# The order of 512-column and 256-column products in the feed-forward projections of a three-layer transformer kernel

## What is computed

```
h = rms_norm(x, g) @ w_up            # 1024 -> 5632
h = depthwise conv of 3 taps over h  # in the first two only (F0, F1)
gate, up = split(h, 2)
x = x + s * (silu(gate) * up) @ w_down   # 2816 -> 1024, s = 1 or 0.5
```

## Time and profile before

| | us |
|---|---|
| three runs | 1035.67, 1035.68, 1037.07 |
| median | 1035.68 |
| span of the profiled execution, first to last instruction | 1034.1 |
| TensorE's products busy | 1007.7 (97%) |
| VectorE busy | 747.2 (72%) |
| ScalarE busy | 626.6 (61%) |
| GpSimd busy | 353.4 (34%) |

### The profile page before, as it was taken

One profiled execution on the slowest core, in us unless ns is written; L12 is line 12 of the kernel. 1 busy time (PEld: TensorE's weight loads), 2 busy tenths in 40 slices (PEclk: granted clock), 3 DMA queues, 4 the chain that ended last, 5 costly groups with the idle time before them and its releaser, 6 DMA issues.

```text
span 1034.1 us, 15900 instructions
## 1 busy us (share of the span) xinstructions
PE 1007.7 (97%) x6476; PEld 903.5 (87%) x6476; DVE 747.2 (72%) x1009; ACT 626.6 (61%) x880; POOL 353.4 (34%) x189
## 2 busy tenths in 40 slices
PE   7999999999998899999999999999999899999997
PEld 7889988888987798888888888888999698888886
DVE  5886999874577789988548766654799887656543
ACT  6776677663477477776436554544669866555531
POOL 1062176640000025665102545510148323555300
PEclk9999999999999999999999999999999999999999
DMA  9633575537441346656553655556342257565341
GB/s 345 223 127 124 220 265 205 199 132 256 147 163 42 121 146 209 238 177 209 190 200 123 244 204 171 195 203 219 122 154 98 83 171 255 184 202 183 144 164 41
DMA packets 27143, 183.45 MB, mean 177 GB/s; under 512 B 3008, under 2 KB 3136, under 8 KB 5824
## 3 DMA queue, kind: packets, MB, share of 16 engines
q1 hardware_dynamic: 26496, 181.40, 49.6%
q10 hardware_dynamic: 576, 1.05, 0.3%
HBM read 181.39 MB, written 1.05 MB: 176 GB/s over the span
## 4 chain that ended last, share of the span: by engine, by line
PE 82%; DVE 8%; ACT 5%; issue 2%; POOL 1%; DMA 1%; SPq 0%; DVEq 0%; POOLq 0%; ACTq 0%
PE psum L335 82%; DVE wlo L1563 2%; ACT whi L1030 1%; POOL Y L2244 1%; ACT Pb L1164 1%; DVE bias L1569 1%; DVE Pb L1694 1%; DMA gain_x<-in_x 1%; DVE Pb L1566 1%; DVE QK L1569 0%; DVE QR L1563 0%; DVE G L1563 0%; DVE Cb L1569 0%; ACT Ob L1372 0%; ACT PT L1030 0%
## 5 line engine op out<-in xcount | busy, mean ns | idle before, releaser
L335 PE MATMUL psum<-G,whi 128*128 128x512 f32 (+1 forms) x1856 | 550.6, 358 | 7.7 <-DVE wlo L1563 7.7
L1563 DVE TENSOR_TENSOR wlo<-raw,whi 128x2048 fp32r<-128x2048 f32 (+1 forms) x170 | 388.2, 2298 | 178.8 <-ACT whi L1030 178.8
L335 PE MATMUL psum<-G,wlo 128*128 128x256 f32 x1568 | 442.0, 282 | 0.0
L1030 ACT ACTIVATE whi<-raw 128x2048 fp32r<-128x2048 f32 (+1 forms) x170 | 315.9, 1871 | 149.5 <-PE psum L335 138.9
L335 PEld LDWEIGHTS psum<-G,whi 128*128 128x128 f32 x1856 | 329.6, 189 | 61.6 <-DVE G L1569 6.4
L335 PEld LDWEIGHTS psum<-G,wlo 128*128 128x128 f32 x1568 | 296.8, 189 | 0.1
L335 PE MATMUL psum<-A2room,whi 128*128 128x512 f32 (+1 forms) x784 | 228.5, 354 | 0.0
L2244 POOL TENSOR_TENSOR A2room<-Ab,A2room 128x512 fp32r<-128x512 f32 x44 | 141.3, 3211 | 130.9 <-ACT A2room L1030 130.9
L335 PE MATMUL psum<-A2room,wlo 128*128 128x256 f32 x656 | 184.6, 281 | 0.0
L335 PEld LDWEIGHTS psum<-A2room,whi 128*128 128x128 f32 x784 | 138.3, 188 | 20.9
L2244 POOL TENSOR_TENSOR Ab<-Cb 128x512 f32<-128x512 f32 x44 | 113.4, 2578 | 107.5 <-ACT Cb L1073 107.1
(11 more groups left out here) (192 smaller groups left out, 1035.9 us busy)
## 6 DMA issues: line engine op xcount, KB each, us to landing
raw<-in_wst SPq DMA_DIRECT2D x165, 1024.0 KB, 5.0
bias<-in_bias_c SPq DMA_DIRECT2D x1, 2048.0 KB, 9.4
raw<-in_wst SPq DMA_DIRECT2D x3, 512.0 KB, 8.1
raw<-in_wst ACTq DMA_DIRECT2D x4, 256.0 KB, 6.2
out<-bias SPq DMA_DIRECT2D x4, 256.0 KB, 2.1
gain_x<-in_x SPq DMA_DIRECT2D x3, 256.0 KB, 6.6
bias<-in_bias_a SPq DMA_DIRECT2D x1, 512.0 KB, 7.5
bias<-in_invcnt SPq DMA_DIRECT2D x1, 512.0 KB, 7.8
```

The lines of the kernel that those rows point to most:

```text
L335: return pe.matmul(o, a, b, start=start, stop=stop, skip_group_check=True)
L1030: return act.activation(o, i, ACT.Copy)
L1563: return dve.tensor_tensor(o, a, b, op)
```

## The change

`wide` gets a range of k-tiles `ks` in place of a half number. For the first output tile it issues all 512-column products, then all 256-column products; for the second the 256-column products first and the 512-column ones behind them. So a whole chunk is eight of 512 columns, sixteen of 256, eight of 512, and the next chunk starts with 512 again. The chunks that were split in two halves stay split. `down_wide` issues, per bank, its two 512-column products and then its two 256-column ones in even banks, and the other way round in odd banks. The products, their operands, the banks and the semaphores that are signalled are the same; the `start` and `stop` flags move to whichever product is now first or last of a bank.

```diff
--- before.py
+++ after.py
@@ -374,23 +374,32 @@
                                          k == 0 and n == 0, k == DT - 1)
                 last.then_inc(s_used, 1)
 
-            def wide(b, i, h, ph=None, normed=None):
-
-
+            def wide(b, i, ks, ph=None, normed=None):
 
                 h3, l3 = weights(i, DT)
-                if h == 0:
+                if ks[0] == 0:
                     pe.wait_ge(s_lo, low_done(i))
-                for n in range(2):
-                    for k in range(4 * h, 4 * h + 4):
+
+                def highs(n):
+                    for k in ks:
                         if n == 0 and ph is not None:
                             pe.wait_ge(s_glo, 8 * ph + k + 1)
-                        if n == 0 and normed is not None:
+                        if n == 0 and normed is not None and k % 4 == 0:
                             pe.wait_ge(s_nlo, 2 * normed + k // 4 + 1)
-                        ws = slice(n * P, n * P + P)
-                        mm(bank[b + n], h3[:, k, ws], G2[:, k, :, :].rearrange("p a s -> p (a s)"), k == 0, False)
-                        last = mm(bank[b + n][:, 0:S], l3[:, k, ws], G2[:, k, 0, :], False, k == DT - 1)
-                if h == 1:
+                        last = mm(bank[b + n], h3[:, k, n * P:n * P + P], G2[:, k, :, :].rearrange("p a s -> p (a s)"),
+                                  k == 0 and n == 0, k == DT - 1 and n == 1)
+                    return last
+
+                def lows(n):
+                    for k in ks:
+                        mm(bank[b + n][:, 0:S], l3[:, k, n * P:n * P + P], G2[:, k, 0, :], k == 0 and n == 1,
+                           k == DT - 1 and n == 0)
+
+                highs(0)
+                lows(0)
+                lows(1)
+                last = highs(1)
+                if ks[-1] == DT - 1:
                     last.then_inc(s_used, 1)
 
             def tokens_first(b, i):
@@ -468,10 +477,14 @@
                         free(b)
                     o = bank[at(ph, b)]
                     ws = slice(b * P, b * P + P)
-                    for kk in range(2):
-                        k = 2 * j + kk
-                        mm(o, h3[:, kk, ws], A2[:, k, :, :].rearrange("p a s -> p (a s)"), k == 0, False)
-                        done = mm(o[:, 0:S], l3[:, kk, ws], A2[:, k, 0, :], False, k == FT - 1)
+                    for high in ((True, False) if b % 2 == 0 else (False, True)):
+                        for kk in range(2):
+                            k = 2 * j + kk
+                            begin, end = k == 0 and high == (b % 2 == 0), k == FT - 1 and high == (b % 2 == 1)
+                            if high:
+                                done = mm(o, h3[:, kk, ws], A2[:, k, :, :].rearrange("p a s -> p (a s)"), begin, end)
+                            else:
+                                done = mm(o[:, 0:S], l3[:, kk, ws], A2[:, k, 0, :], begin, end)
                     if j == FP - 1 and b % 2 == 1:
                         done.then_inc(s_acc, 1)
                 if j < FP - 1:
@@ -502,8 +515,7 @@
                         else:
                             pe.wait_ge(s_ev, 22 * n + 2 * (p - 2) + e + 1)
                         b = at(ph, 4 - 4 * (p % 2)) + 2 * e
-                        for h in range(2):
-                            wide(b, c0 + 2 * p + e, h, None, n if p == NARROW and e == 0 else None)
+                        wide(b, c0 + 2 * p + e, range(DT), None, n if p == NARROW and e == 0 else None)
 
             def up_wide(ph, frees):
                 n = FFNS[ph]
@@ -511,9 +523,9 @@
                 for e in range(2):
                     frees(4 + 2 * e)
                     frees(5 + 2 * e)
-                    wide(at(ph, 4) + 2 * e, c0 + e, 0, ph if e == 0 else None)
+                    wide(at(ph, 4) + 2 * e, c0 + e, range(4), ph if e == 0 else None)
                 for e in range(2):
-                    wide(at(ph, 4) + 2 * e, c0 + e, 1, ph if e == 0 else None)
+                    wide(at(ph, 4) + 2 * e, c0 + e, range(4, DT), ph if e == 0 else None)
                 norm_sum(ph, False)
                 for p in range(1, FP):
                     b = at(ph, 4 - 4 * (p % 2))
@@ -522,8 +534,7 @@
                             pe.wait_ge(s_ev, 22 * n + 2 * (p - 2) + e + 1)
                         elif e == 1:
                             pe.wait_ge(s_rt, ph + 1)
-                        wide(b + 2 * e, c0 + 2 * p + e, 0)
-                        wide(b + 2 * e, c0 + 2 * p + e, 1)
+                        wide(b + 2 * e, c0 + 2 * p + e, range(DT))
 
             def ffn(ph, frees):
```

## The result

The change makes the kernel slower: 1042.28 us median of four runs against 1035.69 us, ratio 1.0055 with a 95% interval of 1.0043 to 1.0067. The forecast was 1030.4 us.

A forecast was written before the change was run, and what follows sets the result against it. TensorE's own pace was taken as the bound. Removing 3184 changes of width at 1.67 ns saves 5.3 us: span 1034.1 to 1028.8, plus 1.6 us distance to the median, 1030.4 us; range 1028.6 to 1036.3 us.

The forecast's parts named there:

- No new wait, no new bound: Whole kernel: same products, transfers and semaphore counts; waits for G, normalized tiles, VectorE and norm's sum costed at nothing.
- the norm's sum: In F2: asked for at 561.16 us, 0.1 us sooner, after GpSimd's last add at 560.17 us; costs nothing.
- The second four tiles of G in F2: F2's wait for G: ready at 554.72 us, asked for after 32 pairs less a little, near 555.6 us; costs nothing.
- the tightest stretch for VectorE: F0's up projection: 86.94 us busy in 94.20, 93% at the new pace; still fits, else 1.8 us of gain lost.
- Three paces: Feed-forward products: alternating pair 346.67 ns, 512 after 512 226.67 ns, 256 after 256 116.67 ns; pure paces add to 343.33 ns.
- the price of two changes of width: Each mixed pair in wide and down_wide: 3.33 ns unaccounted for, taken as 1.67 ns per change of width.
- The count: Changes of width removed: 2392 in wide and 792 in down_wide, together 3184, worth 5.3 us.
- Rival A: 512 products with moving activations simply take 230 ns, so reordering gives nothing: 1035.7 us; chance 0.24.
- My argument against it: Against A: at 256 columns moving activations take 116.67 ns, moving weights 118.3 ns, so moving activations are no slower.
- Rivals B and C: B: 15 ns entry per 512 run, 1033.6 us, chance 0.09; C: entry costs, alternation free, 1038.9 us, chance 0.05.
- The range: Kernel time held 8 in 10: 1028.6 to 1036.3 us, reaching up to A and its scatter.

The follow-up runs named there:

- distance 8: The change itself, buffers left in place: moving activations begin 8 numbers past the weights' place, modulo 128; 1042.28 us, ratio 1.0055 to the kernel before.
- distance 0: New order with G2 and A2 moved by 8 numbers onto the weights' place, against the change; 1043.0 us, ratio 1.0061 to the kernel before.

## Why the prediction was wrong

- **No new wait, no new bound**: right. The waits of TensorE add up to 19.4 us against 19.5; G, the normalized tiles, VectorE and the norm's sum cost nothing, as forecast. Two readings on the way were wrong and did no harm. The second four tiles of G in F2 are asked for after 16 pairs, not 32; the time given, 555.6 us, is that of 16. And the tightest stretch for VectorE before was F1's up projection, 87.88 us busy in 94.20 (93%), not F0's with 86.94.
- **Three paces**: the measurements were right, what I made of them was not, and this is the step that failed. It took the 226.67 ns of F3's down projection as the pace of any 512 behind a 512, and so had 3.33 ns a pair left over, which it called the price of two changes of width. The runs showed the 226.67 to be the pace of operands that lie alike: with F3's standing operand 8 numbers off it is 234 ns. In `wide` G2 lies 8 numbers off `whi`, and there a 512 behind a 512 in a long run takes 233.3 ns, and 228.7 once `whi` or G2 is moved to lie alike. No price of switching was left to remove: at distance 8 alternation is the better order by 3.33 ns a pair.
- **How far that reaches**: it explains the long runs of `wide`, 80 of the 113 chunks. The runs of four in `down_wide` took 350 ns a pair too, but did not get faster when the operands were laid alike (233.5 and 237.1 ns for a 512 behind a 512), so the cause of their 1.8 us stays open. Open too is why alternation escapes the price: at the same distance its 512s take 228.3 and its 256s 118.3 ns, where the distance alone would give 233.3 and 116.7.
- **The count**: 3184 changes of width did go, and 113 chunks carry the loss. It is 6.0 us by pace with the sign turned, 6.6 measured.
- **Rival A** came nearest, and not by its mechanism: there was no price of the switch, but it made the pace a matter of the role of the operand, 230 ns for a 512 with moving activations in any company. Measured are 233.3 in a long run, and 226.7 for the later products of it once `whi` lies like G2. My argument against it compared roles at 256 columns, in the earlier trace rows; the two also differ in the sign of the distance, so it proved nothing about roles.
- **Rivals B and C**: in the run at distance 8 the first products are no slower than the others, so no entry price is needed. At distance 0 there is one, up to 236 ns in the first products after a 256 run, as in the earlier trace rows.
- **The range** ended at A. It took it as certain that the switch costs nothing or more. A run of 512s with moving activations had no row before, and its bound was set downward alone (225 ns, for the range's lower end). Set as far upward, 228.3 ns, it would still have missed. The one row that shows slower 512s is the entry in the earlier trace rows, 0.47 us for two: 235 ns as the pace of every 512 in a run would have given 1030.4 + 1808 x 8.3 ns = 1045.4 us, and a range up to there would have held the result. The forecast's last sentence, that a time above 1036.3 us means a wait or a price in a run, pointed the right way.
- The Trainium skill, "TensorE: Matmul & The Clock Gate", section "Back-to-back issue gap", gives the gap of an isolated product by its columns alone and says that in a stream with weight loads both operations set the spacing; the prediction took the first for the whole. The traces don't agree with the formula: runs of 512 columns took 226.7 to 237 ns a product, not 216, and runs of 256 columns 113.3 to 120 ns, not 109, with the clock full. The Trainium skill, same title, section "Step-by-step: what each phase is for", gives the moving and the standing operand independent read ports. The runs with one of `whi`, `wlo` or `A2last` moved show that the pace depends on how the two lie to each other all the same.

The runs show that in long runs the distance between the moving operand and the weights loaded meanwhile moves the pace, and that what the order is worth depends on it. Not shown is how: a collision of the two reads in the memory would fit, but no run here looks inside. Open also is why one pattern settles on different paces in different stages, and the rule of the short runs in the down projections.

## What to carry to other kernels

Read TensorE's pace from start to start and per pattern of operands, and take a pace from another stage only if roles, widths, the order around the product and the operands' places (here modulo 64 numbers) are the same too. When TensorE is the bound and shows no waits, try the offset between moving and standing operands together with the order: here the four combinations of order and offset 8 or 16 lie between 1034.0 and 1044.7 us, and an order that loses at one offset wins at the other. Tune them as a pair, by measurement, and again after any change to either.

## What the runs showed of the hardware

- A product of 512 columns of this type, its successor's weights loaded meanwhile, takes 226.7 to 237 ns and one of 256 columns 113.3 to 123 ns, at the full granted clock, by the distance of the two operands in SBUF and by the order of the products around it. In the new order 32 bytes of distance (16 numbers in place of 8) were worth 8 us of this kernel.
- A repeating pattern can settle on one of two paces with the same code and the same places modulo 128: 353.3 ns a pair in F0 and 346.7 in F1, F2 and F3 of one execution.
- Moving the activation buffers by 8 numbers a step changes the time of kernels that compute the same in the same order: 1042.3 us at 8, 1034.0 at 16, 1051.8 at 24 (a single run).
